# Storing the second tile's gates in one transfer of 128 tokens instead of two of 64

## The reference

```python
def peer_ffn(h, w_query, sub_keys, expert_u, expert_v):
    q = (x @ w_query).reshape(T, PEER_HEADS, 2, PEER_HALF)
    s1 = einsum('thd,kd->thk', q[:, :, 0], sk[0]); s2 = einsum('thd,kd->thk', q[:, :, 1], sk[1])
    v1, i1 = top_k(s1, 16); v2, i2 = top_k(s2, 16)
    sc, flat = top_k(all sums v1 + v2, 16)          # e = i1 * 128 + i2, the expert
    g = softmax(sc)                                 # the gate of each picked expert
    a = gelu(x . expert_u[e]);  y = sum over picks of g * a * expert_v[e]
```

## Time and profile before

| | us |
|---|---|
| median of three runs | 1598.76 (1597.06 to 1599.52) |
| the profiled execution, its own time | 1599.17 |
| its span | 1597.2 |
| PE busy | 1501.3 (94%) |
| DVE busy | 1337.7 (84%) |
| POOL busy | 804.4 (50%) |
| ACT busy | 668.0 (42%) |
| mean granted TensorE clock | 0.978 of full speed |
| bytes moved | 447.58 MB, mean 280 GB/s |

### The profile page before, as it was taken

How to read it: one execution, slowest core, us unless ns; L and a number is a source line. 1 busy time by engine, 2 the same in 40 slices (tenths; PEclk the granted TensorE clock), 3 DMA queues, 4 the chain that set the end, 5 groups by cost and what they waited for, 6 DMA issues and landing times.

```text
span 1597.2 us, 25315 instructions
## 1 busy us (share of the span) xinstructions
PE 1501.3 (94%) x7879; PEld 1279.6 (80%) x7879; DVE 1337.7 (84%) x2628; ACT 668.0 (42%) x1213; POOL 804.4 (50%) x757
## 2 busy tenths in 40 slices
PE   4999999999998958699999999999999999999996
PEld 3678776685777747588999999999999999999995
DVE  5777634452899889889999999999999999999998
ACT  4332445412127754444444444434444444444443
POOL 1000000001009978677766766767667667667662
PEclk8999999999999969999999999999999999999998
DMA  9975211232011437999999999999999999999994
GB/s 347 391 255 199 93 53 53 89 127 104 1 54 71 114 76 222 212 364 405 406 405 397 404 379 389 405 361 400 399 370 400 390 374 406 382 376 406 376 390 163
DMA packets 212878, 447.58 MB, mean 280 GB/s; under 512 B 80235, under 2 KB 98947, under 8 KB 212556
## 3 DMA queue, kind: packets, MB, share of 16 engines
q1 hardware_dynamic: 156620, 242.08, 42.9%
q0 software_dynamic: 56192, 204.66, 32.7%
HBM read 423.78 MB, written 22.32 MB: 279 GB/s over the span
## 4 chain that ended last, share of the span: by engine, by line
PE 79%; DVE 9%; issue 4%; DMA 3%; POOL 2%; ACT 2%; SPq 0%; POOLq 0%; DVEq 0%; ACTq 0%
PE bank L908 14%; PE bank L1114 8%; PE bank L1115 8%; PE bank L1113 8%; PE bank L1137 7%; PE bank L1135 7%; PE bank L1136 7%; PE bank L1127 3%; PE bank L1128 3%; PE bank L1062 3%; PE bank L845 2%; PE bank L1074 2%; DMA w_scratch<-staged 2%; PE bank L1011 2%; POOL hot L780 1%
## 5 line engine op out<-in xcount | busy, mean ns | idle before, releaser
L1113 PE MATMUL bank<-h_hi,u_hi 128*128 128x320 f32 x960 | 297.4, 310 | 8.7 <-DVE u_lo L1952 8.7
L753 POOL DMA_INDIRECT v_rows<-v_exp,small x192 | 256.7, 1337 | 91.2 <-POOL small L749 51.8
L753 POOL DMA_INDIRECT u_rows<-u_exp,small x192 | 254.9, 1328 | 93.1 <-POOL small L749 52.0
L1114 PE MATMUL bank<-h_lo,u_hi 128*128 128x320 f32 x960 | 298.0, 310 | 0.0
L1115 PE MATMUL bank<-h_hi,u_lo 128*128 128x320 f32 x960 | 298.0, 310 | 0.0
L1464 ACT ACTIVATE v_hi<-v_raw 128x1024 fp32r<-128x1024 f32 x128 | 135.4, 1058 | 170.1 <-PE bank L1137 170.1
L1137 PE MATMUL bank<-v_hi,g_both 128*128 128x512 f32 x512 | 203.9, 398 | 0.0
L1135 PE MATMUL bank<-v_hi,g_both 128*128 128x512 f32 x512 | 202.7, 396 | 0.0
L1136 PE MATMUL bank<-v_lo,g_both 128*128 128x512 f32 x512 | 202.7, 396 | 0.0
L1113 PEld LDWEIGHTS bank<-h_hi,u_hi 128*128 128x128 f32 x960 | 181.3, 189 | 13.8 <-issue 8.9
L1114 PEld LDWEIGHTS bank<-h_lo,u_hi 128*128 128x128 f32 x960 | 181.2, 189 | 6.2
(11 more groups left out here) (250 smaller groups left out, 2973.2 us busy)
## 6 DMA issues: line engine op xcount, KB each, us to landing
v_raw<-v_exp SPq DMA_DIRECT2D x128, 512.0 KB, 7.9
u_raw<-u_by_key SPq DMA_DIRECT2D x120, 512.0 KB, 5.9
ada_blk<-ada_w SPq DMA_DIRECT2D x22, 1024.0 KB, 10.1
ring<-w_in SPq DMA_DIRECT2D x18, 1024.0 KB, 5.2
w_scratch<-staged SPq DMA_DIRECT2D x4, 4096.0 KB, 24.4
w_row<-w_scratch SPq DMA_DIRECT2D x128, 128.0 KB, 9.2
xr<-x SPq DMA_DIRECT2D x8, 512.0 KB, 6.0
ring<-w_branch SPq DMA_DIRECT2D x4, 1024.0 KB, 5.0
```

What stands on the lines that cost most here:

```text
L753: pool.indirect_dma_start(out=rows[s], out_offset=None, in_=table, in_offset=bass.IndirectOffsetOnAxis(ap=ix[:, s:s + 1], axis=0))\
L1113: pe.matmul(o, u_hi[:, r, k], h2_hi[:, k], start=(k == 0), stop=False)
L1114: pe.matmul(o, u_hi[:, r, k], h2_lo[:, k], start=False, stop=False)
```

## The change

The two stores of tile 1, tokens 0 to 63 and 64 to 127, become one of tokens 0 to 127. It is issued once all 32 groups of tile 1 are staged, where the second store was issued. The three waits on `w_stored[1]` ask for one completion (16) instead of two (32). Bytes and the places in memory are the same; the runs in memory are 512 B long instead of 256 B. Tile 0's stores stay as they are.

```diff
@@ -656,9 +656,8 @@
             for q in range(STEP):
                 load_units(q, q)
                 load_values(q, q)
-            store_gates(1, 0, EX, w_stored[1])
-            store_gates(1, EX, P, w_stored[1])
-            sp.wait_ge(w_stored[1], 32)
+            store_gates(1, 0, P, w_stored[1])
+            sp.wait_ge(w_stored[1], 16)
             for q in range(STEP):
                 load_gates(q, q)
 
@@ -796,7 +795,7 @@
-            pool.wait_ge(w_stored[1], 32)
+            pool.wait_ge(w_stored[1], 16)
             for part in range(2):
                 gather_u(0, part)
@@ -1495,7 +1494,7 @@
-            act.wait_ge(w_stored[1], 32)
+            act.wait_ge(w_stored[1], 16)
             act.wait_ge(w_staged, ALL_GROUPS)
```

## The result

The changed kernel takes 1602.43 us (median of 12 runs, 1600.50 to 1604.81) against 1599.03 us before (12 runs, 1596.88 to 1601.74): 3.4 us more, ratio 1.0021 with a 95% interval of 1.0013 to 1.0029. It is slower, by about the least that can be told from no change. Forecast was 1597.8 with a range up to 1602.2; the forecast had the wrong sign, and the time is just beyond the range.

The account below looks back on a forecast made before the run. Tile 1's second store, exposed before the PE-bound dense loop, was taken to set the loop's start. -6.44 us of queueing and +5.51 us of larger packets gave -0.9 us, a median of 1597.8 us, range 1594.6 to 1602.2.

Parts of the forecast that it names:

- What bounds the kernel: Before the dense loop: tile 1's second store alone holds POOL, ACT and SP, so its landing shifts the whole loop.
- The 27.64 us: Tile 1's second store: 21.20 us as a store alone plus 6.44 us queued behind the first store.
- Added: the first half's bytes: Merged store after 647.53: 16,384 packets of 512 B at 24.2 ns, 26.7 us in all, +5.51 us against before.
- a line through packets that overlap: Merged store's packet cost, interpolated from 14.42 ns at 256 B and rows of 2 and 4 KB: 24.2 ns at 512 B.
- the upper bound: Merged store's packets not overlapping: 27.8 ns busy plus at most a 0.87 ns gap, 28.6 ns per 512 B packet.
- break-even: Cost of a 512 B packet at which the merged store lands as late as before: 25.1 ns.
- a fixed pace: At the DMA engines: packets handed over no faster than one in 18.8 ns; with a backlog 256 B takes 14.4 ns.
- rival B: Packets of a store alone don't overlap: 27.8 to 28.6 ns, landing 2.7 to 3.6 us later, 1601.5 to 1602.4; chance 0.21.
- The sum: Landing of tile 1's store: -6.44 us of queueing gone, +5.51 us for larger packets, together -0.9 us.
- Rival A: Every packet costs 18.8 ns, 256 or 512 B: store lands at 668.7, time 1592.3 to 1593.2 us; chance 0.14.
- Rival C: Merged store keeps runs of 256 B: 32,768 packets, 38.5 us and more, 12.8 us slower; chance 0.03.
- PE's clock: Before the loop PE resumes at 1.2 of 2.4 GHz; effect of the shift put at zero, within half a us.

Follow-up runs that it names:

- experiment 1: Kernel before the change, with tile 1's first store also held back until all of tile 1 is staged: 1612.46 us, ratio 1.0090.
- Experiment 5: Kernel before the change, with tile 0's second half in two stores, the first issued near 590 on idle DMA engines: 1592.49 us, ratio 0.9960.
- the quarters: Kernel before the change, with tile 1 in four stores of 32 tokens, runs of 128 B: 1612.86 us in one execution.
- experiment 2: Changed kernel with the eight loads of 512 KB moved behind the wait for staging, ahead of the merged store: 1612.99 us in one execution.

## Why the prediction was wrong

**What bounds the kernel** was right. The store of tile 1 stands alone between the last staging and the loop, and the shift passes on almost whole: from SP's first gate load to the end of the span it was 922.0 us before, 921.6 after, and 920.3 in experiment 1, with the load at 675.2, 679.7 and 691.7.

**The 27.64 us** were taken apart rightly: 21.20 us of a store alone and 6.44 of queueing. Experiment 5 removed the second part and got 21.13.

**The step that failed** is the cost of a 512 B packet in "Added: the first half's bytes". It said 24.2 ns, by a line through packets that overlap. Measured are 28.2 ns, against the upper bound of 28.6 and a break-even of 25.1. The line itself was good: 23.5 ns behind loads. What was wrong was to use it for a store that starts on idle engines. Of the two states in the trace, (a store alone, 95.4%, 18.8 ns) was the state in which the changed store would be, and the earlier trace rows (127.7%, 14.4 ns) was a store behind loads. I carried the second over by a mechanism, packets handed over at a fixed pace and an engine that catches up when there is a backlog. Runs of 128 B at 11.8 ns refute the fixed pace. Against the backlog speak the stores behind large stores, which waited 3.4 and 3.7 us and ran at 18.8 ns from their first packets; with as long a wait as behind loads it was not tried. The text named this as rival B ("the overlap at 640 may owe to the loads ahead") and gave it 0.21; its argument against, that no load's packet is left in 640 to 643, showed only that the state outlives the loads by some microseconds.

**The sum with the right price** is -6.44 + 1,024 x (28.2 - 18.82) ns = +3.2 us. The landing moved by 30.64 - 27.64 = 3.0, the median by 3.4.

**Rival B** had the right price, in part by luck. It was called "packets of a store alone don't overlap", and took 27.8 ns of busy time plus a gap of up to 0.87. The trace shows a share of 103.3%, so 1.033 x 28.2 = 29.1 ns busy per packet, and packets that overlap a little; with 128 B they overlap by far (165%). So the line through busy times was too low, and the gap that was added to it is not there.

**Rival A** (18.8 ns for either size) was refuted: 290 GB/s, not 435. The page "DMA: Bandwidth & Descriptors" of the Trainium skill, under "Specifications", puts the least size for line rate at 512 B; the trace doesn't agree, for stores of 512 B rows ran at 290 GB/s against 401 with rows of 4 KB. **Rival C** (runs cut to 256 B) fell too: all packets are of 512 B.

**PE's clock.** I put its effect at zero. In the changed kernel the chain behind the landing runs over ACT, DVE and PE instead of POOL, with PE at 1.2 GHz; 685 to 686 still has 0.50 granted. But the lower level ends some 8 us behind the landing in both kernels (full speed is granted from 683 to 684 before, 0.94 from 687 to 688 after). The loop's remainder, 921.6 us against 922.0, shows no cost.

**The range** reached to 1602.2 and should have held all of B with its scatter; 0.2 us were missing.

## What to carry to other kernels

Before merging two transfers, ask when the last of their bytes becomes available: what the first one moved under other work cost nothing here, and the merged one moves it in the open. Price the merged transfer by a row in the same state as it will be in (alone, behind loads, behind stores), since the same packet took 17% (512 B) to 23% (256 B) less behind loads than alone. And where the exposed transfer queues behind an earlier one, look upstream for idle DMA time: here a store split in three, with more packets in all, gained nearly twice what the merge lost (6.2 against 3.4 us).

## What the runs showed of the hardware

Time per packet and engine of stores from the core's memory, in the states seen:

| run of | alone | behind loads, at first |
|---|---|---|
| 128 B | 11.8 ns (about 9.4 in the first 1.5 us) | 11.8 ns (about 9.0 in the first 1.5 us) |
| 256 B | 18.8 ns | 14.4 ns |
| 512 B | 28.2 ns | 23.5 ns |

The first row is from the kernel of experiment 5 (174 GB/s from 594 to 600, 218 from 592 to 592.5) and from the quarters (173 and 227 GB/s). Behind stores only runs of 256 B were measured: 18.8 to 18.9 ns, as alone.

From 256 to 512 B both columns rise by 9.1 to 9.4 ns. Lines through these two sizes leave a fixed part of about 9.4 ns alone and about 5 behind loads, an estimate that 128 B doesn't bear out.

The page "DMA: Bandwidth & Descriptors" of the Trainium skill, under "Why small descriptors are slow (HBM only)", names a fixed cost of about three cycles beside the 32-byte beats. An estimate with its 850 MHz: 28.2 ns are 24 cycles for 16 beats, eight more than the beats, and 23.5 ns are 20, four more. So the page's figure nearly fits the state behind loads; alone it is more than twice as much. No run here shows in what these cycles lie.

The quick state lasts for some 10 to 14 us after the last load, fading towards its end, and then ends by itself: until about 647 in the kernel before, 667 behind four loads, 674 in experiment 2. Why, and what sets its length, stays open, and so does whether a store that waits longer behind stores would show it. Packets of 128 B overlap by themselves (share 165%) and are cheaper than the line of the larger ones; loads ahead change them little.
